# Layers' gate product: sixteen plain tiles become four plain tiles and six pairs of seven block products

## What is computed

```python
h = h + jnp.concatenate([ya, yb], axis=-1) @ w_out[i]
e = _rmsnorm(p[i] @ w_pe[i], pe_g[i])
h = h + e * jax.nn.sigmoid(h @ w_pg[i])     # the gate: (512 x 2048) @ (2048 x 2048)
```

## Time and profile before

| | |
|---|---|
| median of 3 runs | 2524.61 us (2524.43 to 2525.24) |
| the profiled execution | 2524.99 us |
| its span, first to last instruction | 2523.2 us |
| PE busy | 2515.8 us |
| gate stage of the first layer, on PE | 711.27 to 885.80 us |
| gate stage of the second layer, on PE | about 1588.9 to 1763.4 us |

### The profile page before, as it was taken

The page is one execution under the profiler, slowest core; times in us unless marked ns, Lnnn a source line. Parts: engine busy times, 40 slices in busy tenths (PEclk is TensorE's granted clock), DMA queues, the critical chain, the costliest instruction groups (busy, mean ns, idle before and its releaser), DMA issues.

```text
span 2523.2 us, 40982 instructions
## 1 busy us (share of the span) xinstructions
PE 2515.8 (100%) x15264; PEld 2130.5 (84%) x15264; DVE 1549.4 (61%) x2510; ACT 1066.7 (42%) x1618; POOL 1324.5 (52%) x1668
## 2 busy tenths in 40 slices
PE   9999999999999999999999999999999999999999
PEld 7888888889988888888878899888888888899887
DVE  7977766575462387777665745634654655955722
ACT  6212365643462342223655434634322656545421
POOL 6555554443355555555454434555666776534554
PEclk9999999999999999999999999999999999999999
DMA  7322243248733333223432487233322323388322
GB/s 251 114 92 99 97 123 113 91 144 210 165 108 125 116 118 101 98 94 101 120 114 95 162 188 171 92 133 114 112 98 94 101 92 100 98 188 241 101 95 105
DMA packets 95424, 313.56 MB, mean 124 GB/s; under 512 B 9456, under 2 KB 25584, under 8 KB 92208
## 3 DMA queue, kind: packets, MB, share of 16 engines
q1 hardware_dynamic: 75264, 268.45, 31.6%
q0 software_dynamic: 10368, 37.75, 8.6%
q10 hardware_dynamic: 9648, 5.36, 1.0%
HBM read 297.86 MB, written 16.81 MB: 125 GB/s over the span
## 4 chain that ended last, share of the span: by engine, by line
PE 99%; DMA 0%; ACT 0%; DVE 0%; issue 0%; SPq 0%; POOL 0%; DVEq 0%; ACTq 0%
PE acc L2070 18%; PE acc L2071 18%; PE acc L2072 17%; PE sc L2071 6%; PE sc L2070 6%; PE sc L2072 6%; PE sc L2340 2%; PE sc L2341 2%; PE sc L2342 2%; PE acc L2340 1%; PE acc L2341 1%; PE acc L2342 1%; PE acc L2094 1%; PE sc L2094 1%; PE sc L2096 1%; PE sc L2100 1%
## 5 line engine op out<-in xcount | busy, mean ns | idle before, releaser
L792 POOL TENSOR_TENSOR WL<-raw,WH 128x256 fp32r<-128x256 f32 x1504 | 1195.0, 827 | 907.6 <-ACT WH L852 907.3
L2070 PE MATMUL acc<-XH,WH 128*128 128x512 f32 x1936 | 756.4, 391 | 0.1
L2071 PE MATMUL acc<-XL,WH 128*128 128x512 f32 x1936 | 753.7, 389 | 0.0
L2072 PE MATMUL acc<-XH,WL 128*128 128x512 f32 x1936 | 753.3, 389 | 0.0
L852 ACT ACTIVATE WH<-raw 128x1024 fp32r<-128x1024 f32 x378 | 398.9, 1058 | 795.2 <-PE acc L2072 538.6
L2070 PEld LDWEIGHTS acc<-XH,WH 128*128 128x128 f32 x1936 | 363.4, 188 | 80.5 <-issue 4.9
L2072 PEld LDWEIGHTS acc<-XH,WL 128*128 128x128 f32 x1936 | 363.5, 188 | 76.0
L2071 PEld LDWEIGHTS acc<-XL,WH 128*128 128x128 f32 x1936 | 363.5, 188 | 74.3
L2070 PE MATMUL sc<-XH,WH 128*128 128x512 f32 x640 | 249.0, 389 | 0.0
L2071 PE MATMUL sc<-XL,WH 128*128 128x512 f32 x640 | 249.0, 389 | 0.0
L2072 PE MATMUL sc<-XH,WL 128*128 128x512 f32 x640 | 249.0, 389 | 0.0
(11 more groups left out here) (425 smaller groups left out, 4408.3 us busy)
## 6 DMA issues: line engine op xcount, KB each, us to landing
raw<-in_w SPq DMA_DIRECT2D x416, 512.0 KB, 3.3
raw<-in_w POOLq DMA_DIRECT2D x54, 512.0 KB, 6.2
a<-in_w POOLq DMA_DIRECT2D x18, 512.0 KB, 5.9
a<-in_w SPq DMA_DIRECT2D x16, 512.0 KB, 7.6
h_spill<-H SPq DMA_DIRECT2D x8, 1024.0 KB, 6.1
H<-h_spill SPq DMA_DIRECT2D x8, 1024.0 KB, 8.2
a<-bias_band SPq DMA_DIRECT2D x16, 384.0 KB, 3.7
H<-in_x SPq DMA_DIRECT2D x5, 1024.0 KB, 7.6
```

What stands on the lines that cost most here:

```text
L792: part = pool.tensor_tensor(WL[:, c], raw[:, c], WH[:, c].bitcast(F), ALU.subtract)
L2070: pe.matmul(bank, WH[:, c], xh, start=first, stop=False)
L2071: pe.matmul(bank, WH[:, c], xl, start=False, stop=False)
L2072: return pe.matmul(bank, WL[:, c], xh, start=False, stop=last)
```

## The change

PLAIN = 4 gate tiles stay as they were, but in two banks, G[0] and G[1], since the four others are taken by sums: PE may start tile 2 when ACT's tanh of tile 0 has read its bank. The other 12 tiles are six pairs in the 42 steps of W_STEPS. The halving goes into the tanh (scale=0.5). Where Y held e, the sums now lie, so e goes to DRAM (e_spill, four stores of 1 MB) and comes back tile by tile (16 loads of 256 KB, into acc, rs and at the end Y); h is stored in 16 transfers of 256 KB and not four of 1 MB. Of each pair's seven low weight parts DVE makes six and POOL one (p2). `stat` moves from behind the second tile to the middle of it.

```diff
-A_U, KV_U, Z_U, OUT_U, PE_U, PG_U = 48, 8, 32, 8, 4, 32
+A_U, KV_U, Z_U, OUT_U, PE_U, PG_U = 48, 8, 32, 8, 4, 8
...
+def side_kinds(g):
+    return ("p2",)
...
@@ GpSimd, after the units of the embed and of the four plain tiles
+                block_weights(ly)
...
+                    if kind in side_kinds(g):
+                        pool.wait_ge(fast_high, fast_base(g) + j + 1)
+                        for k in range(LOW_PARTS):
...
+                        part.then_inc(side_low, 1)
+                    if w_next(j) is not None and not w_loads(w_next(j)):
+                        pool.wait_ge(*w_low_made(g, j))
+                        pool.dma_start(W_PLACE[name], w[w_unit(g, *W_STEPS[w_next(j)])], accum_op=ALU.add)...
@@ ScalarE
                 split_high(4 * ly + 3)
+                for c in range(4):
+                    act.wait_ge(e_kept[c], 16 * (ly + 1))
+                sum_highs(0)
+                third_high(0)
+                third_high(1)
                 prep(u0, PG0 + 2)
+                root(rs[:, :], ly * 4 + 4, 4.0 / D)
+                sum_highs(1)
+                gate(0)
+                sum_highs(2)
                 prep(u0, PG0 + 3)
-                root(rs[:, :], ly * 4 + 4, 4.0 / D)
                 gate(1)
+                sum_highs(3)
+                block_prep(0)
                 square(0)
+                square(1)
+                block_prep(1)
+                gate(2)
...
+                block_prep(2)
+                square(2)
+                gate(3)
+                for j in range(3, W_N + RING):
+                    if j < W_N:
+                        block_prep(j)
+                    else:
+                        act.wait_ge(fast_used, pg0 + j - RING + 1)
+                        prep(u0, PG0 + RING + j - W_N)
+                    if 4 <= j < 6:
+                        third_high(j - 2)
+                    if j == 5:
+                        square(3)
...
@@ VectorE
-                halve(0)
-                halve(1)
+                sum_adds(0)
+                third_add(0)
+                third_add(1)
+                sum_lows(0)
+                third_low(0)
+                third_low(1)
+                sum_adds(1)
+                sum_adds(2)
+                sum_lows(1)
+                sum_adds(3)
+                sum_lows(2)
                 dve.wait_ge(root_ready, ly * 3 + 3)
                 did(dve.reciprocal(ers[:, :], rs[:, :]))
+                sum_lows(3)
                 settle()
                 scaled(0)
                 gated(0)
                 scaled(1)
                 gated(1)
+                block_lows(0)
+                sums(0)
+                sums(1)
+                scaled(2)
+                gated(2)
...
+                block_lows(2)
+                sums(2)
+                for j in range(W_N):
+                    for n in SPLITS:
+                        if j == g_done(n) + 4:
+                            sums(n)
+                    if j:
+                        block_outs(j - 1)
+                    if j + 3 < W_N:
+                        block_lows(j + 3)
...
+                        if j == g_done(n) + 2:
+                            gated(n)
...
+                        if j == g_done(n) + 1:
+                            scaled(n)
...
@@ TensorE
-                quad_tile(n0 + N_PG, u0 + PG0, 0, x0 + 2 * NT)
-                quad_tile(n0 + N_PG, u0 + PG0, 1)
-                stat(4 * ly + 3)
...
+                for t in range(PLAIN):
+                    if t >= 2:
+                        pe.wait_ge(g_th, ly * NT + t - 1)
+                    unit(u0 + (PG0 + 2 * t), 2 * t % RING, 0, G[t % 2], None if t else x0 + 2 * NT)
+                    if t == 1:
+                        stat(4 * ly + 3)
+                    unit(u0 + (PG0 + 2 * t + 1), (2 * t + 1) % RING, 1, G[t % 2], None if t else x0 + 2 * NT)
...
+                for j, (kind, q) in enumerate(W_STEPS):
...
+                    pe.wait_ge(*w_low_made(ly, j))
+                    if back is not None:
+                        pe.wait_ge(fast_out, fast_base(ly) + back + 1)
...
+                        pe.matmul(bank, WH[:, c], gate_moving(kind, k, False), ...)
+                        pe.matmul(bank, WH[:, c], gate_moving(kind, k, True), ...)
+                        last = pe.matmul(bank, WL[:, c], gate_moving(kind, k, False), ...)
```

More of the change, by code:

```diff
@@ L743, in _ @@
+                for n in (NT - 4, NT - 3):
+                    h_store(n)
+                units(u0, LAYER_U, LAYER_U + RING, skip=skip)
+                for n in (NT - 2, NT - 1):
+                    h_store(n)
+            skip = DEPTH * (SKIP_U + W_SKIP)
             units(B0, 4, RG0 - RING - B0, skip=skip)
@@ L1108, in _, with sum_highs, third_high @@
                 split_high(4 * ly + 3)
+                pg0 = fast_base(ly)
+                s0 = 16 * ly
+                def sum_highs(c):
+                    for i, which in enumerate((1, 2)):
+                        act.wait_ge(sum_whole, s0 + sums_begun(c) + i + 2)
+                        act.activation(sums_of(which, False)[:, 2 * c:2 * c + 2, :], two(sum_banks(c)[i]), ACT.Copy).then_inc(sum_head, 1)
+                def third_high(c):
+                    act.wait_ge(sum_whole, s0 + (4 + c if c < 2 else 13 + c))
+                    if c >= 2:
+                        act.wait_ge(sum_tail, s0 + 14)
+                    act.activation(p_third(False, c), two(TR[c if c < 2 else 0]), ACT.Copy).then_inc(sum_head, 1)
@@ L1153, in xc_high @@
+                for t in range(UT, NT):
+                    if t == UT + 2:
+                        square(NT - 1)
+                    xhigh(t, tl(H, t), norm_col(ly + 1, t))
             def xc_high(g):
@@ new lines, in block_outs @@
+                def block_outs(j):
+                    kind, q = W_STEPS[j]
+                    bank = XB_OF[bank_of(kind, q)]
+                    parts = rows_of(kind)
+                    row, half = parts[0]
+                    before = [w_rows_before(j, part) for part in parts]
+                    to = tl(T, 2 * (q % 2) + row)
+                    c = slice(half * HALF, (half + 1) * HALF)
+                    for i in before:
+                        if i is not None:
+                            dve.wait_ge(fast_out, pg0 + i + 1)
+                    if None in before:
+                        n = PLAIN + W_ORDER.index((q, row))
+                        dve.wait_ge(hsum_ready, ly * NT + NT + place_before(n) + 1)
+                    dve.wait_ge(fast_used, pg0 + j + 1)
+                    if kind == "p5" and before == [None, None]:
+                        both = bass.AP(bank, 0, [[S, P], [0, 2], [1, HALF]])
+                        dve.tensor_scalar(two(to), both, -1.0, None, ALU.mult).then_inc(fast_out, 1)
+                    elif kind == "p5":
+                        assert before[1] is None
+                        did(dve.tensor_tensor(to[:, 0:HALF], to[:, 0:HALF], bank[:, 0:HALF], ALU.subtract))
+                        settle()
+                        dve.tensor_scalar(to[:, HALF:S], bank[:, 0:HALF], -1.0, None, ALU.mult).then_inc(fast_out, 1)
+                    elif before[0] is None:
+                        dve.tensor_scalar(to[:, c], bank[:, 0:HALF], 1.0 if kind in ("p1", "p2", "p4") else -1.0, None,
+                                          ALU.mult).then_inc(fast_out, 1)
+                    else:
+                        dve.tensor_tensor(to[:, c], to[:, c], bank[:, 0:HALF],
+                                          ALU.add if kind in ("p1", "p2", "p4") else ALU.subtract).then_inc(fast_out, 1)
@@ L1766, in _ @@
+                block_outs(W_N - 1)
+                sums(NT - 3)
+                scaled(NT - 1)
+                next_low(4)
+                next_low(5)
+                gated(NT - 1)
+                sums(NT - 2)
+                for k in range(6, 10):
+                    next_low(k)
+                sums(NT - 1)
+                for k in range(10, NT):
+                    next_low(k)
             xb = DEPTH * 3 * NT
```

453 lines of the change are left out of this document (299 added, 154 removed).

## The result

The changed kernel takes 2550.73 us (median of four runs, 2550.16 to 2552.77) and the kernel before 2524.74 us (2524.43 to 2525.24): a ratio of 1.0104, 95% interval 1.0087 to 1.0122. The forecast was 2530 us with a range to 2543. Slower was the likeliest of the three outcomes by the text (0.47), but the time lies 7.7 us above the range.

What follows compares the result with a forecast made beforehand. The prediction took PE, busy 100% of the span, as the bound. It summed -19.2 (PE work) + 15.8 (start holes) + 1.4 + 3.0 (pair steps) + 1.5 (DMA) + 1.0 + 2.0 (end) = +5.5 us: 2530 us, range 2517 to 2543.

Steps and rivals of the forecast that it cites:

- PE's rate: Gate stages: pair-step matmuls at 0.1200 us replace plain ones at 0.2267 us, saving 9.6 us a layer, 19.2 in all.
- (a): Start of the gate stage: PE reaches the moved `stat` before its input, the split, is ready and idles 2.0 us.
- (b): Ahead of plain tile 2: PE waits for ACT's first tanh, which frees tile 0's bank, and idles 4.5 us.
- (c): Pair step 6: its low part ends a chain through DVE, ACT and POOL; PE waits 1.0 us, second layer 1.8.
- The sum of the start: Holes at `stat`, tile 2 and step 6: 7.5 and 8.3 us by layer, together 15.8 us of the 19.2 saved.
- D, the clock: Rival: the 4.5 us hole brings a 1.2 GHz clock for one unit, 5.4 us more a layer less 1.0; 2539, chance 0.09.
- The pair steps: In the pair steps DVE's in-order list comes late at some steps, losing 1.4 us in the first layer, 3.0 in the second.
- DMA: Pair steps: added loads and stores leave little idle and make landings later; 1.5 us taken in all.
- rival C: DMA bounds the pair steps: PE waits once landings take about 9 us; at 10 us, 8 us a layer; 2546, chance 0.05.
- The end: Start of the next stage: its unit 1 comes 1.0 us late in the first layer, 2.0 us in the second.

Runs made afterwards that it cites:

- e8: Changed kernel with `stat` moved back behind the second plain tile, as in the kernel before; 2551.75 us.
- e1: Changed kernel with ScalarE's tanh of plain tile 0 put ahead of its first two copies of sums; 2551.06 us.
- e7: Changed kernel with four moves: first tanh earlier, step 6's high part earlier, `stat` back behind the second plain tile, h stored behind the pair steps; 2542.70 us.
- e3: Changed kernel with e loaded back as only 16 columns a tile (h multiplied in its place) and h stored behind the pair steps; 2537.43 us.
- e4: Changed kernel with VectorE's `scaled`, `gated` and sums of the pair tiles on 64 of 512 columns, all transfers kept; 2547.74 us.
- e11: Changed kernel with 28 unread matmuls of 16 columns ahead of the first layer's tile 2, shifting PE's later instructions; 2544.69 us in one run.
- e5_late_h: Changed kernel with only the twelve stores of h moved behind the pair steps, e coming back as before; 2543.98 us.
- e2_fill: Changed kernel with unread matmuls on PE in the holes, 8 ahead of `stat` and 20 ahead of tile 2 in each layer; 2548.00 us.

## Why the prediction was wrong, step by step

- *PE's rate* (19.2 us saved): right. Undisturbed steps of the changed kernel are 2.88 us, and steps 7 to 26 of the first layer take 54.74 us where 19 x 2.88 = 54.72.
- *(a) and (b)*: the holes were right in place, releaser and size (1.9 for 2.0; 3.1 and 4.7 for 4.5). In the first layer the hole ahead of tile 2 is shorter by what the low clock behind `stat` took: tile 2 began at the same distance from the split (11.65 us) in both layers. Priced as costs of their own they were not right: e8 took one away and got nothing back, e1 and e7 got back 1.0 to 1.8 us a layer, in the second layer no more than the spread.
- *(c)*: right in kind, and the sentence that "a shorter hole in (b) would come back in (c)" is what e1 and e7 showed. That step 6 waits 1.0 us in the first layer, as forecast, is partly luck: counted from the stage's start, GpSimd began its low part 0.4 us later than forecast and took 4.79 us in place of 2.9 to 3.15, and PE came there 2.3 us later than forecast. In the second layer e's return for tile 2 was taken at 0.6 us and cost VectorE a wait of 4.13, and a wait of 1.0 us at step 3 was not foreseen.
- *The sum of the start* (15.8 us, measured 24.8): all waits of PE ahead of step 7 sum to 16.2 us, so the holes as such were forecast well. What was missing is the low clock behind them, 7.2 us; the remaining 1.4 us were not traced. The text put it at nothing in its sum.
- *D, the clock* (chance 0.09): it is this missing term. The prediction treated it as an alternative to the forecast; a cost that follows from the holes belonged into the sum with them. Its price there was 5.4 us a layer less the 1.0 that step 6 waits; the low clock slowed matmuls by 3.3 and 3.9 us a layer ahead of step 7, and by 2.8 us at step 37.
- *The pair steps* (4.4 us by VectorE's list) *and DMA* (1.5 us): this is the step that failed most. The text put the slips on VectorE and named DMA as a small addition with the rival C behind it. The runs have it the other way round: with the extra transfers away the steps lose 0.3 and 0.9 us from step 7 on (e3), with VectorE's extra work away they lose 6.3 and 6.3 (e4). By e3 DMA's term was 11.5 us (12.7 - 1.2), for 1.5; in the six kernels with the same steps the whole loss is 10.4 to 19.6 us. The reading of a share of 0.84 plus 15% as "little idle" was right; the 1.5 us were taken and not worked out from it, and the loss comes from single landings (10.2 us at step 37) where the text had a median of 6.2.
- *C, DMA becomes the bound* (2546, chance 0.05) is therefore the rival that was closest in kind: its price was 8 us a layer, and 11.5 us in two layers came. Its condition, landings of more than about 9 us, is what step 37 met.
- *The end*: 0.2 and 2.9 us for 1.0 and 2.0: right in sum, less so by layer. In the second layer PE waits 1.7 us at the next stage's first matmul; the profile names no releaser, and the wait ends when GpSimd's four pieces of the unit's low part are made.
- *Outside the gate stage* nothing was forecast and 5 us were lost: 2.6 us in the attention (e11) and 2.5 us at the third block's steps 37 and 38. The latter steps have the code they had; step 37's weight part landed 5.5 us after its issue before and 7.1 us after it now. Before, that left 1.4 us of room. The experiments lose from 0.1 to 3.4 us there, and why was not settled.

No version here beats the kernel before. The best with the whole computation and four runs, e7_all, stands at 2542.7 us, with e5_late_h beside it; what is left in it is 8.9 and 13.2 us ahead of step 7, mostly VectorE's list, 2.0 and 3.9 us from step 7 on, and some 8 us at the next stages' starts, in the attention and in the third block, and the saving on PE is 19.2.

## What to carry to other kernels

In this case the holes of PE showed where VectorE's list was first waited for, not what they cost: before pricing a hole, ask what the same list is waited for next, and whether that moves. Judge transfers that are added to a stage by the latest landing that its chain can bear, as step 37 shows, not by the median landing; and count a low clock with the holes that bring it, not as an alternative to them.

## What the runs showed of the hardware

- In the changed kernel the granted clock fell to 0.50 in five places, for 3.4 to 6.8 us each, at the end of holes of PE of 1.9 to 4.7 us or just behind them, and not at others (1.9 and 1.7 us in the second layer). In the eight kernels that keep the hole of 1.9 us ahead of `stat` it fell behind 10 of 16 such holes. With the holes filled by idle matmuls (e2_fill) it stayed at 1.00 in those places.
- GpSimd and VectorE can take longer beside each other. GpSimd's four pieces of a low part took 2.83 us at 1695.0 of the changed kernel with VectorE idle, and 4.8 us in the two places where VectorE worked nearly throughout; with 2.1 us of VectorE's work beside them they took 2.80 (at 1715.2). A sum of VectorE of 0.7 us took 3.9 us in e7_all while GpSimd made such a low part (from 773.90, 3.15 us):

```profile
773.68 3.94 DVE L1909 TENSOR_TENSOR tr<-H 128x512 f32<-128x512 f32 x1
```

- PE stopped for 0.9 to 1.7 us, twice, in untouched code, in ten kernels, and for 0.4 us in the two that have 28 PE instructions more ahead of that place. What it stops for is open.
